# First mixer's projections as three terms of split operands, with keys, norm sums, turning and filter in another order

## What is computed

```python
mod_l = jnp.split(s_lat @ ada_w[i] + ada_b[i], N_MOD, axis=-1)
a_lat = _modulate(_rmsnorm(h_lat, norm1_g[i]), mod_l[0], mod_l[1])
a_ctx = _modulate(_rmsnorm(h_ctx, norm1_g[i]), mod_c[0], mod_c[1])
p_lat = a_lat @ mix_w_in[e] + mix_b_in[e]            # q, k, v and 3 x 512 for hyena
q_l = _axial_rope(_split_q(p_lat), row, col)
k_l, v_l = _split_kv(p_lat[..., KV_START:HY_START]); k_l = _axial_rope(k_l, row, col)
kv_ctx = a_ctx @ mix_w_in[e][:, KV_START:HY_START] + mix_b_in[e][KV_START:HY_START]
att_l = _diff_post(_diff_attn_blocked(q_l, k_all, v_all, lam), subln_g[e], lam_init)
# hyena: short convolution of 3 taps on each stream, then
return x0 * _long_conv(v * x1, filt, bias)           # rfft(u) * rfft(filter), irfft
y_lat = jnp.concatenate([att_l, hy_l], axis=-1) @ mix_w_out[e] + mix_b_out[e]
h_lat = h_lat + mod_l[2] * y_lat
```

## Time and profile before

| | |
|---|---|
| median of 3 runs | 2473.55 us (2471.55 to 2474.41) |
| profiled execution, its time | 2470.5 us |
| profiled execution, its span | 2468.7 us |
| TensorE busy | 2337.3 us, 95% of the span |
| VectorE, ScalarE, GpSimd busy | 1002.4, 611.2, 121.4 us |
| mean granted clock of TensorE | 0.985 |
| share of the last chain | PE 80%, DMA 14%, DVE 3% |

### The profile page before, as it was taken

One profiled execution on the slowest core, in us unless ns is written; L12 is line 12 of the kernel. 1 busy time (PEld: TensorE's weight loads), 2 busy tenths in 40 slices (PEclk: granted clock), 3 DMA queues, 4 the chain that ended last, 5 costly groups with the idle time before them and its releaser, 6 DMA issues.

```text
span 2468.7 us, 24555 instructions
## 1 busy us (share of the span) xinstructions
PE 2337.3 (95%) x10377; PEld 1404.9 (57%) x10377; DVE 1002.4 (41%) x1607; ACT 611.2 (25%) x991; POOL 121.4 (5%) x128
## 2 busy tenths in 40 slices
PE   6999989999999999999999999999898998989888
PEld 3445544788888888888877758344333333323322
DVE  4655572566664665665676465111111010101011
ACT  3112162423323333233456463001010100000000
POOL 2000000000000000000221331100000000000000
PEclk9999999999999999999999999999999999999999
DMA  9322230355553155551320215899999999999998
GB/s 369 111 69 85 103 137 34 128 194 174 203 188 102 51 185 190 197 195 36 91 69 27 89 65 238 357 431 430 430 431 430 431 430 431 430 431 430 431 430 343
DMA packets 124403, 594.11 MB, mean 241 GB/s; under 512 B 10898, under 2 KB 12448, under 8 KB 98950
## 3 DMA queue, kind: packets, MB, share of 16 engines
q1 hardware_dynamic: 120866, 583.18, 59.6%
q0 software_dynamic: 3120, 9.24, 1.1%
q10 hardware_dynamic: 308, 0.13, 0.0%
HBM read 590.39 MB, written 2.14 MB: 240 GB/s over the span
## 4 chain that ended last, share of the span: by engine, by line
PE 80%; DMA 14%; DVE 3%; ACT 1%; issue 0%; SPq 0%; POOL 0%; DVEq 0%; ACTq 0%
PE PS L1309 15%; PE PS L984 9%; PE PS L986 9%; PE PS L985 9%; PE PS L1037 7%; PE PS L777 6%; PE PS L176 5%; PE PS L1331 4%; DMA RING<-in_w_down_dram 2%; PE PS L1346 2%; PE PS L943 2%; DMA RING<-in_w_gate_dram 2%; PE PS L863 2%; PE PS L640 2%; DMA RB_a<-in_w_up_dram 1%; DMA RB_a<-in_w_down_dram 1%
## 5 line engine op out<-in xcount | busy, mean ns | idle before, releaser
L1309 PE MATMUL PS<-RING,HID_e 128*64 128x512 f32 x576 | 205.8, 608 | 9.4 <-DMA RING<-in_w_gate_dram 5.4
L1309 PE MATMUL PS<-RB_a,HID_e 128*64 128x512 f32 x576 | 204.5, 605 | 8.2 <-DMA RB_a<-in_w_up_dram 5.6
L2705 DVE TENSOR_TENSOR TMP<-TMP,PS 128x512 f32<-128x512 f32 x32 | 19.8, 682 | 370.9 <-PE PS L1309 370.9
L1309 PE MATMUL PS<-HID_e 128*64 128x512 f32 x320 | 145.8, 605 | 5.8 <-DMA HID_e<-in_w_gate_dram 2.6
L1309 PE MATMUL PS<-AT_g,HID_e 128*64 128x512 f32 x288 | 130.3, 601 | 7.2 <-DMA AT_g<-in_w_up_dram 4.6
L1309 PE MATMUL PS<-XT,HID_e 128*64 128x512 f32 x288 | 128.6, 595 | 5.4 <-DMA XT<-in_w_up_dram 2.7
L1895 ACT ACTIVATE HID_e<-PS,cmat 128x128 f32<-128x128 f32 x32 | 12.1, 456 | 463.4 <-PE PS L176 463.4
L1309 PEld LDWEIGHTS PS<-RING,HID_e 128*64 128x64 f32 x576 | 63.2, 139 | 95.2 <-issue 78.6
L1309 PEld LDWEIGHTS PS<-RB_a,HID_e 128*64 128x64 f32 x576 | 61.2, 139 | 93.6 <-issue 79.7
L1331 PE MATMUL PS<-RB_a,HID_e 128*64 128x512 f32 x288 | 99.6, 625 | 11.8 <-DMA RB_a<-in_w_down_dram 11.8
L1331 PE MATMUL PS<-RING,HID_e 128*64 128x512 f32 x304 | 102.6, 602 | 7.4 <-DMA RING<-in_w_down_dram 7.4
(11 more groups left out here) (466 smaller groups left out, 4670.9 us busy)
## 6 DMA issues: line engine op xcount, KB each, us to landing
RING<-in_w_gate_dram SPq DMA_DIRECT2D x18, 2048.0 KB, 22.1
RB_a<-in_w_gate_dram SPq DMA_DIRECT2D x18, 2048.0 KB, 22.0
RB_a<-in_w_up_dram SPq DMA_DIRECT2D x18, 2048.0 KB, 18.0
RING<-in_w_down_dram SPq DMA_DIRECT2D x18, 2048.0 KB, 22.0
RB_a<-in_w_down_dram SPq DMA_DIRECT2D x18, 2048.0 KB, 22.1
RING<-in_w_up_dram SPq DMA_DIRECT2D x17, 2048.0 KB, 17.2
RING<-in_mlp_w_dram SPq DMA_DIRECT2D x32, 1024.0 KB, 5.2
RB_a<-in_mlp_w_dram SPq DMA_DIRECT2D x32, 1024.0 KB, 5.2
```

The costliest lines, as they stand in the source:

```text
L1309: last = pe.matmul(b[64 * d:64 * d + 64, :], xv_[:, k, 64 * d:64 * d + 64], wv, start=k == 0, stop=k == 7)
```

## The change

The projections of the first mixer (three hyena streams, queries, keys, values) become parts 0 to 5 of the machinery that the second mixer uses, whose own parts are now numbered from M = 6. Context keys, filter, tables and rotation stay f32. In detail:

- The normalised input is written twice by ScalarE, once as f32 (`norm_x`) and once rounded to float32r (`AH3`, in the place of `AT`); VectorE subtracts to `AL3`. The context's normalised input gets a high part `ACXH` (ScalarE) and a low part `ACXL` (GpSimd), each in one instruction.
- 48 slices of weights pass ScalarE and GpSimd. `RB` is taken by `AL3`, `WPH` and `WPL`, so the ring has four slots until the values are through.
- VectorE does the filter's decay before the taps of stream 1, and half of the filter's transform is combined between the blocks of stream 2.
- TensorE does four slices of the keys before the convolution, and the other four around the context's norm sums and the turning of the queries. The turning works from `PADS` instead of `TMP`. All four key blocks are turned after the first block of context keys.
- The values run slice by slice over six banks at once; the bias comes in VectorE's eviction, from a row loaded onto all partitions, and ScalarE evicts no values.
- Of the adaLN blocks 8 to 11, accumulation moves behind the attention, into the output projection, and one joint sum and turn (`pe_ada_four`, `pe_ada_turn`) replaces four column sums.
- The norm's squares of the output projection, the adaLN steps and the first two MLP weight splits are interleaved on ScalarE and VectorE.

The core of the diff:

```diff
-        brow = sb("brow", [1, 512 + 32])
+        brow = sb("brow", [128, 512 + 32])
+        ACXH, ACXL = lay_out("h", *MIXER[0:3], ("LOW", (128, 8192), F32), ("ACXH", (128, 8, 256), F32R),
+                             ("ACXL", (128, 8, 256), F32R))[4:]
...
+        parts = [(T_hy, "hy", 1), (T_hy, "hy", 2), (T_hy, "hy", 0), (T_qkv, "q"), (T_qkv, "k"), (T_qkv, "v"),
+                 (T_ml, "xm"), (T_ml, "so"), (T_ml, "av"), (T_dil, "ak"), (T_dil, "aq"), (T_out, "out2", 0),
+        M = 6
...
+            ring.many, ring.i = 4, 0
+            sp_part(sp, w, Win, 0, 2048)
+            sp_ada(sp, w, 0, 4)
+            sp_part(sp, w, Win, 1, 2560)
+            sp_ada(sp, w, 0, 5)
+            sp_part(sp, w, Win, 2, 1536)
             ring.load(sp, w, ("ctx",), A["ctx"][0].rearrange("(t p) d -> p t d", p=128), (2, 1024), (T_hy, "ctx", 7))
+            sp_part(sp, w, Win, 3, 0)
+            sp_ada(sp, w, 0, 6)
+            sp_part(sp, w, Win, 4, 512, (T_qkv, "kc", 3))
+            sp_part(sp, w, Win, 5, 1024)
             sp_ada(sp, w, 0, 7)
+            ring.many, ring.i = NSLOT, 4
+            for b in range(4, 8):
+                ring.freed[b] = ((T_qkv, "v", 5),)
...
+            ks = pe_open(pe, w, 4, lambda j: ((S_qkv, "rk", j),), (4, 5, 6, 7))
+            pe_parts(pe, w, 4, ks, range(4), AH3, AL3, fed0)
             w.wait_ge(*V_hy.at("comb", 1, 3))
...
+            pe_parts(pe, w, 4, ks, (4,), AH3, AL3, fed0)
+            banks.i = 0
             pe_norm_cols(pe, w, 1, 256)
+            for j in range(4):
+                pe_rotate(pe, w, "rq", j, 1 + j % 3)
+            pe_parts(pe, w, 4, ks, (5,), AH3, AL3, fed0)
+            pe_norm_spread(pe, w, 1, 256)
+            pe_parts(pe, w, 4, ks, (6, 7), AH3, AL3, fed0)
...
+            for k in range(6):
+                for i in range(6):
+                    last = group(k, i)
+                last.then_inc(*T_prt.up(5, k))
+            for i in range(6):
+                group(6, i)
+                group(7, i).then_inc(*T_qkv.up("v", i))
...
+                if j == 3:
+                    pe_ada_four(pe, w, 0, 2)
                 products(1, j, open_bank(1, j), (4, 5, 6, 7, 0, 1, 2, 3))
+            pe_ada_turn(pe, w, 0, 2)
...
+                act.activation(x, AT[:, k, :], ACT.Identity, bias=mod0[:, k:k + 1, 0], scale=g1s[:, k:k + 1]).then_inc(
+                    *S_nrm.up("x", 0, k))
+                act.activation(AH3[:, k, :], AT[:, k, :], ACT.Identity, bias=mod0[:, k:k + 1, 0],
...
+            act.activation(ACXH[:, :, :], ACX, ACT.Copy, bias=0.0, scale=1.0).then_inc(*S_qkv.up("acxh"))
+            high(5, 0, 1)
             for j in range(4):
-                q = act_tmp.take(w, ("rk", j), (V_qkv, "rk", j, 2))
+                q = pads.take(w, ("rk", j), (V_qkv, "rk", j, 2))[:, 0:512]
...
+            for i in range(6):
+                w.wait_ge(*T_qkv.at("v", i))
+                dve.tensor_tensor(Vt[:, i, :], banks.of("v", i), brow[:, 0:512], ALU.add).then_inc(*V_qkv.up("v", i))
...
         def dve_out1(dve, w):
+            dve_ada(dve, w, 0, 8)
+            dve_ada(dve, w, 0, 9)
...
+                if jj == 3:
+                    dve_ada(dve, w, 0, 10)
+                elif jj == 4:
+                    dve_ada(dve, w, 0, 11)
+                    dve_split(dve, w, 0, 0)
+                    dve_split(dve, w, 0, 1)
```

More of the change, by code:

```diff
@@ L434, in sp_pair, with sp_part @@
                 ring.load(sp, w, (*label, kh), rows_of(W, 4 * kh, c0), (4, 512), *freed)
+        def sp_part(sp, w, W, b, c0, *more):
+            for kh in range(2):
+                ring.load(sp, w, (*parts[b][1:], kh), rows_of(W, 4 * kh, c0), (4, 512), (G_prt, b, 4 * kh + 3), *more)
         def sp_ada(sp, w, which, cb):
@@ L519, in sync_program @@
             for b, c0 in enumerate((0, 512, 2064, 1552, 1040, 0, 512)):
-                W = W2in if b < 5 else A["w_out_2"][0]
-                for kh in range(2):
-                    ring.load(sp, w, (*parts[b][1:], kh), rows_of(W, 4 * kh, c0), (4, 512), (G_prt, b, 4 * kh + 3))
+                sp_part(sp, w, W2in if b < 5 else A["w_out_2"][0], M + b, c0)
                 if b == 1:
@@ L853, in pe_qkv @@
                 if j == 0:
[L854 to L866 removed]
+                    for i in range(4):
+                        pe_rotate(pe, w, "rk", i)
+            pe_ada_sum(pe, w, 6)
+            pe_values(pe, w)
             b = banks.take(w, ("lam",), (S_qkv, "lam"))
@@ L1413, in act_part @@
             if n < 4:
+                w.wait_ge(*T_set.at("ada", 7))
+            elif b == M and k < 4:
                 w.wait_ge(*V_mlp.at("lo", 1, 31))
@@ L2158, in dve_hyena, with part @@
         def dve_hyena(dve, w):
-            def part(n):
-                for j in range(4):
+            def part(n, js=range(4)):
+                for j in js:
                     ct = 4 * n + j
```

426 lines of the change are left out of this document (223 added, 203 removed).

## The result

The changed kernel takes 2457.3 us (median of 4 runs, 2453.48 to 2458.75), the kernel before 2473.98 us over its 4 runs: the ratio is 0.9928, with a 95% interval of 0.9914 to 0.9943. It is faster by 16.7 us, where 29.7 were forecast; the time lies in the range, and 13.3 us above the forecast of 2444. The profiled execution took 2456.2 us.

What follows compares the result with a forecast made beforehand. The first mixer was taken as one long TensorE queue that bounds the kernel. The terms -47.5 + 3.5 + 1.7 + 9.5 + 1.7 + 1.4 = -29.7 us gave a median of 2444 us, range 2429 to 2460.

Steps and rivals of the forecast that it cites:

- rival 2: Feeding engines delay each other: 47 us on VectorE, or ScalarE stands before the third part; 2449 to 2459 us, chance 0.22.
- What goes: First mixer on TensorE: cheaper split products, value bias matmuls and four adaLN column sums gone; -47.5 us together.
- The start: First products wait for a cut slice and split activations, +3.5 us; lower clock after that idling, +1.7 us.
- The filter's tables: Around the hyena filter's tables: late weights and eviction were to cost 0, up to 5 us if anything slips.
- After the convolution: Serial chain until the first key block is turned: 28.1 us against TensorE's 18.6, +9.5; lower clock, +1.7.
- The output projection: Four adaLN blocks move here; TensorE gains a joint sum and turn, loses some waiting: +1.4 us (0 to 5).
- the sign that it named: GpSimd subtractions in the first mixer taking 2 us and more on average would say the port.
- The rule of the Trainium skill: A VectorE instruction with both inputs in SBUF and a GpSimd instruction reading SBUF exclude each other for their whole length.
- Rival 3: Slices set the pace at 3.5 us or more each, slower than before; 2483 us at 3.7, chance 0.03.
- Rival 4: Split products no cheaper because weight loads come exposed, losing 37.7 us of savings; 2472 us, chance 0.04.
- Rival 1: Gaps do not open, loads land at once and the chain overlaps: -44.8 us, 2429 us, chance 0.19.
- the three gaps: TensorE waits before the column sums, norm spreading and key turning behind the convolution: some 2.6, 2.7 and 4.2 us.

Runs made afterwards that it cites:

- evict_first: Changed kernel with ScalarE evicting the second hyena part before it cuts the first two slices of the third; 2452.31 us.
- narrow_low: Changed kernel with GpSimd subtracting only 64 of 512 columns per slice from the second part on, output not the reference's; 2450.73 us.
- moved_narrow: adaln_moved with GpSimd subtracting only 64 of 512 columns from the second part on, output not the reference's; 2435.26 us against 2432.08.
- double_low: Changed kernel with GpSimd subtracting every slice twice from the second part to the values, same result; 2486.48 us, ratio 1.0044 to the kernel before.
- adaln_moved: Changed kernel with evictions before slices, four subtractions before table loads, norm chain reordered, adaLN block 6 and block 4's sum moved; 2432.08 us.

## Why the prediction was right, and where it was off

It was right in kind: faster, through cheaper products, with chains that take some of it back. The forecast itself, 2437 to 2451 us with its gaps within 7 us, was missed; 2457.3 lies where rival 2 had it (2449 to 2459, chance 0.22), and the range holds because it took in that rival. By its steps:

**What goes** (-47.5): right. A part takes 22.06 us in place of 21.8, which is some 1.1 us over five parts; the values take the forecast 32.8.

**The start** (+3.5 and +1.7): 3.1 and 2.3, the latter since eleven products take the 4.8 us from 43.72 to 48.55 and would take 2.5 at full clock. The size of the first came by two errors that cancel: GpSimd's issues began 0.9 us earlier than in before (39.45, the weights had landed sooner), and its first subtraction took 1.70 us in place of 1.30, beside VectorE's subtractions of 1.42 to 1.77 (0.69 alone). GpSimd's table issues were on the path: in the four kernels that have them behind four subtractions the first product came 0.3 to 1.5 us earlier.

**The filter's tables** (0, up to 5): this is the step that failed. It cost 0.95 + 3.99 + 0.61 us of waits and 2.0 of low clock, 7.6 us, more than its bound and two thirds of all that was missing. The chain had been written down right (VectorE's adaLN block, the load, two slices, the eviction), with 34 us against TensorE's 35. The eviction came 40 us after the start of the filter products, because VectorE's block ended after 29.9 in place of 26 us and the load took 8.2 in place of 5.2. A cover of one microsecond on a sum of five serial terms was taken as cover. With the evictions ahead of the slices the wait of 3.99 us is gone (evict_first), and without most of GpSimd's work it is 1.97 (narrow_low). Why the load took longer was not tried.

**After the convolution** (+9.5 and +1.7): waits of 7.4 us, low clock of 5.0; the sum is 12.4 in place of 11.2. The waits were smaller (7.4 for 9.5), the low clock behind them cost three times as much: it came after two of them where the sum had the last alone, and the last cost 3.1 us in place of 1.7. One term is misnamed: the 2.4 us are three steps of adaLN block 6, not four, and three are what frees a slot (block 4 starts at 93.67, SyncE issues into its first slot at 96.01).

Small waits of 0.85 and 0.41 us ahead of the queries and the values were not in the sum. Together, from start to values: 0.2 + 1.1 + 7.6 + 1.2 + 1.3 = 11.4 us to the scores. **The output projection** (+1.4) gave 1.3 (148.07 us from the scores to the MLP, 146.78 before). The rest is the 3.8 us lost behind the MLP's start, of which 2.2 are shown to be clock.

**The rivals.** Rival 2 was right in both its mechanisms, VectorE that loses time to GpSimd and ScalarE that stands before the third part, and the time lies in its range. Its price of 47 us on VectorE was too high: 27 go with GpSimd's columns. The time is no measure of the port alone either, since with the queues in another order the same loss on VectorE costs nothing (moved_narrow). The evidence had been read on the wrong engine: the prediction looked at the length of GpSimd's subtractions (median 1.30 us) and found hardly any conflict. These rows don't show what VectorE did beside them, and the sign that it named, subtractions of 2 us and more on average, did not come (1.48); the length of VectorE's steps is where it shows. The rule of the Trainium skill, page "SBUF — State Buffer", section "Who interferes with whom", gave this case. The runs here agree (27 us of VectorE's busy time go with GpSimd's columns). The page adds that the order of issue decides which of the two stands, which no run here tested. And the trace of before had it, in the second mixer, where GpSimd already subtracts; VectorE's timeline there, alone and beside a subtraction at 1254.87:

```profile
1251.39 0.54 DVE L2469 TENSOR_SCALAR TMP<-PADS,VC 128x512 f32<-128x512 f32 x1
...
1255.00 1.52 DVE L2469 TENSOR_SCALAR TMP<-PADS,VC 128x512 f32<-128x512 f32 x1
```

Rival 3, slices that set the pace, is out: behind the first product no wait of over 0.3 us ends with a slice. Even with doubled subtractions only one does (0.38 us), so that double_low comes near this rival's 2483 us by another path, through VectorE. Rival 4 is out, the products cost 0.23 us each. Rival 1 is out for the changed kernel, where the three gaps opened; adaln_moved came near its 2429 us (2432.08), by another order of the queues.

## What to carry to other kernels

When work is taken off the engine that bounds, list what every in-order queue has in front of the instructions that free its buffers: an eviction that needs nothing should not stand behind a slice that needs a load. Each of the two such swaps here moved one line and gave 5 to 7 us, where the whole change gave 17. And when a new stream of work goes onto GpSimd, read VectorE's durations beside GpSimd's in the trace one already has, and give VectorE's chains the longer steps in the sum.

## What the runs showed of the hardware

A GpSimd subtraction of 128 x 512 in SBUF (median 1.30 us) often lengthens VectorE's step beside it by about 0.9 to 1.1 us, also for an operation with a single tensor input (TENSOR_SCALAR, 0.54 to 1.52 us), and not for those that read one operand from PSUM (0.68 us throughout). GpSimd can stand too: at the start each of four took 1.69 to 1.73 us. Behind TensorE's waits of 5.02, 3.99, 2.65 and 3.84 us the lower clock (0.50, 0.66, 0.67 and 0.50 granted) cost another 2.3, 2.0, 1.9 and 3.1 us, so that the edit which removed the wait of 3.84 us gave 6.2 us from the convolution's first product to the scores, and 7.1 in the median. Behind those of 0.61, 0.85 and 0.95 us the granted clock was 1.00.
